# Sixteen dense products, which nothing reads, at the head of each step of the last mixers with a recurrent chunk

## What is computed

```
def _dsa_mixer(q, c, iq, ik, iw, w_uk, rel_bias):      # per block of 128 queries
    dots = jnp.einsum('bqhd,bsd->bqhs', iqb, ik) * idx_scale
    score = jnp.einsum('bqh,bqhs->bqs', iwb * w_scale, jax.nn.relu(dots))
    score = jnp.where(admissible[None], score.astype(jnp.float32), -jnp.inf)
    _, sel = lax.top_k(score, k_sel)                    # 256 keys of up to 2048
...
    logits = (jnp.einsum('bqhr,bqkr->bqhk', ql, c_sel).astype(jnp.float32) * scale
              + jnp.swapaxes(bias, -1, -2).astype(jnp.float32))
    p = jax.nn.softmax(logits, axis=-1).astype(c.dtype)
    return jnp.einsum('bqhk,bqkr->bqhr', p, c_sel)

def _hgrn2_mixer(q, f_raw, v, lb):                      # per chunk, with a carried state
    scores = jnp.einsum('bhtk,bhsk,bhtsk->bhts', qn, kn, decay)
    o = (jnp.einsum('bhts,bhsv->bhtv', scores, vn)
         + jnp.einsum('bhtk,bhkv->bhtv', qn * jnp.exp(bn), state))
    state = (jnp.exp(b_last[:, :, 0, :])[..., None] * state
             + jnp.einsum('bhsk,bhsv->bhkv', kn * jnp.exp(b_last - bn), vn))
```

## Time and profile before

| what | value |
|---|---|
| time, median of 3 runs | 5533.85 us (5530.03 to 5535.99) |
| time of the profiled execution | 5534.45 us |
| its span in the profile | 5532.8 us |
| mean granted TensorE clock | 0.837 of full speed |
| TensorE, VectorE, ScalarE busy over the span | 82%, 47%, 34% |
| steps k = 0 to 15 of the last mixers | 3719.6 to 5197.8 us, 27% of the span |

### The profile page before, as it was taken

The page is one execution under the profiler, slowest core; times in us unless marked ns, Lnnn a source line. Parts: engine busy times, 40 slices in busy tenths (PEclk is TensorE's granted clock), DMA queues, the critical chain, the costliest instruction groups (busy, mean ns, idle before and its releaser), DMA issues. The chain is left out here.

```text
span 5532.8 us, 59862 instructions
## 1 busy us (share of the span) xinstructions
PE 4531.4 (82%) x20858; PEld 3279.3 (59%) x20858; DVE 2604.0 (47%) x5329; ACT 1896.7 (34%) x3847; POOL 689.8 (12%) x724
## 2 busy tenths in 40 slices
PE   3994999984478888989798999966688877877689
PEld 3883777774367677777445888853344444545544
DVE  3011444454555554444111111127898888888433
ACT  3011322233322332333111101013677767777511
POOL 3001111110000000000000000003223333444300
PEclk7997999996687877777899999976577887877699
DMA  3514666664100000000322121120000001011032
GB/s 126 167 64 150 215 215 209 206 219 137 40 32 22 22 22 13 20 22 3 112 87 82 63 80 68 65 73 12 25 20 18 18 18 35 18 35 35 31 135 87
DMA packets 227869, 417.63 MB, mean 75 GB/s; under 512 B 36905, under 2 KB 100041, under 8 KB 227401
## 3 DMA queue, kind: packets, MB, share of 16 engines
q1 hardware_dynamic: 227568, 413.81, 22.2%
HBM read 292.08 MB, written 121.65 MB: 75 GB/s over the span
## 5 line engine op out<-in xcount | busy, mean ns | idle before, releaser
L2382 PE MATMUL ds_big<-ds_ikT,ds_iqT 64*128 64x512 f32 (+3 forms) x640 | 385.5, 753 | 88.0 <-ACT ds_iqT L2359 57.0
L2893 POOL TENSOR_TENSOR ds_E<-ds_bT 128x256 f32<-128x256 f32 x112 | 72.1, 643 | 2966.3 <-ACT ds_bT L2862 2782.7
L292 DVE COPY g_stage<-g_acc 128x512 f32<-128x512 f32 (+2 forms) x96 | 61.6, 642 | 784.9 <-PE g_acc L280 784.9
L278 PE MATMUL g_acc<-g_ws_hi,second_hT_hi 128*128 128x512 f32 (+1 forms) x1024 | 385.0, 376 | 11.7 <-DVE g_ws_lo L313 11.7
L279 PE MATMUL g_acc<-g_ws_lo,second_hT_hi 128*128 128x512 f32 (+1 forms) x1024 | 384.7, 376 | 0.0
L280 PE MATMUL g_acc<-g_ws_hi,second_hT_lo 128*128 128x512 f32 (+1 forms) x1024 | 384.6, 376 | 0.0
L549 PE MATMUL mm_big<-mm_gw_hi,mm_ghT_hi 128*128 128x512 f32 (+1 forms) x768 | 318.8, 415 | 43.2 <-PEq L134 42.7
L2445 DVE TENSOR_SCALAR_CACHE_REDUCE ds_eq<-ds_hi,ds_num 128x2048 uint16<-128x2048 uint16 (+13 forms) x224 | 331.3, 1479 | 25.3 <-issue 3.0
L306 ACT ACTIVATE g_stage<-g_acc 128x512 f32<-128x512 f32 (+2 forms) x96 | 53.7, 559 | 844.5 <-PE g_acc L280 844.5
L551 PE MATMUL mm_big<-mm_gw_hi,mm_ghT_lo 128*128 128x512 f32 (+1 forms) x768 | 300.4, 391 | 0.0
L550 PE MATMUL mm_big<-mm_gw_lo,mm_ghT_hi 128*128 128x512 f32 (+1 forms) x768 | 299.3, 390 | 0.0
(11 more groups left out here) (498 smaller groups left out, 9894.3 us busy)
## 6 DMA issues: line engine op xcount, KB each, us to landing
mm_ghT_hi<-turned SPq DMA_DIRECT2D x96, 512.0 KB, 4.2
mm_ghT_lo<-turned SPq DMA_DIRECT2D x96, 512.0 KB, 5.6
proj<-g_stage SPq DMA_DIRECT2D x160, 256.0 KB, 2.0
g_w<-in_w_in SPq DMA_DIRECT2D x80, 256.0 KB, 4.0
proj<-mm_gstage SPq DMA_DIRECT2D x80, 256.0 KB, 5.0
mm_x<-proj SPq DMA_DIRECT2D x64, 256.0 KB, 3.9
mm_graw<-in_w_in SPq DMA_DIRECT2D x40, 256.0 KB, 6.2
po_m<-mixed SPq DMA_DIRECT2D x16, 640.0 KB, 4.7
```

Of the source, the lines that this page charges most:

```text
L278: pe.matmul(sums, hT.hi[:, k, tile], wt.hi[:, k, 0:width], start=(k == 0), stop=False)
L2382: pe.matmul(big[:, n % 2, 0:wd], iqT[o, h // 2], b.ikT[o, x:x + wd], start=True, stop=True)\
```

## The change

A helper `dense` issues sixteen products on TensorE. Each takes the first 128 columns of the constants, read as bfloat16, as weights, and 512 columns of the same tile, read as bfloat16, as the moving operand, and writes all 512 columns of a bank of PSUM. Nothing waits for them, they wait for nothing, and nothing reads what they write. In `second_mixers` it is called ahead of all other work of TensorE in the steps k = 0 to 15, with bank 7 of `big`; in each of these steps that bank is written anew (L2972) before it is read.

```diff
+DENSE = 16
+
+
+def dense(pe, c, bank):
+
+
+    half = c.all[:, 0:GROUP // 2].bitcast(BF16)
+    for _ in range(DENSE):
+        pe.matmul(bank, half[:, 0:P], half, start=True, stop=True)
...
                 @block.tensor
                 def _(pe):
+                    if k < TILES:
+                        dense(pe, c, big[:, 7])
                     together(pe, "tensor", branches)
```

## The result

| | before | with the change |
|---|---|---|
| median of the runs timed together | 5534.92 us (4 runs) | 5579.77 us (4 runs, 5575.79 to 5591.14) |
| ratio | | 1.0086, 95% interval 1.0070 to 1.0102 |
| timed again, beside the last experiments | 5532.66 us (23 runs) | 5579.86 us (6 runs), ratio 1.0086 (1.0071 to 1.0101) |
| profiled execution, span | 5532.8 us | 5574.8 us |

The kernel is 0.86% slower, by 45 to 47 us. The forecast was 5579 us.

What follows compares the result with a forecast made beforehand. VectorE's list was taken to fill a step, its head hanging on a TensorE-ScalarE relay. ScalarE's 53 us less 11.5 slack gave 42, taken as 45; with 0 for k = 0 to 2, 5579 us, range 5550 to 5608 (8 in 10).

Steps and rivals of the forecast that it cites:

- The head is a relay, and the burst stands ahead of it: Heads of k = 3 to 15: TensorE and ScalarE wait on each other, so the burst delays ScalarE by 53 us in all.
- cold heads: 8 of the 13 heads, met at 1.2 GHz: burst 6.0 us, 1.4 given back, ScalarE 4.6 us later each.
- warm ones: 5 of the 13 heads, met at 2.4 GHz: burst 4.2 us, 0.9 given back, ScalarE 3.3 us later each.
- The give-back: L2692 and L2697 behind the burst run at 2.4 GHz: 1.4 us saved in a cold head, 0.9 in a warm one.
- The slack ahead of L2942 is taken off: VectorE starts L2942 after L2851 has ended; this slack, 11.5 us over 13 steps, cuts its delay from 53 to 42 us.
- Nothing takes the delay back: Behind L2942 VectorE is nearly full, so its 42 us delay reaches the step's end; later waits may raise it, at most to 53.
- k = 0 to 2 count nothing: The three steps before: slack of 7.9 and 4.7 us hides the burst in k = 1 and 2; k = 0 counts 0, 3 us either way.
- The warm head: Rival: the clock stays up until the chunk's products, some 15 us behind the entry, giving 5500 to 5526 us; chance 7%.
- Absorption: Rival: VectorE's slack and later waits in the step soak up the delay, 0 to 11 us, 5534 to 5545 us; chance 8%.
- the clock that does not rise: Rival: the burst's mostly zero operand does not raise the clock, bursts take 6.9 us, nothing given back, 5612 us; chance 8%.

## Why the prediction was right, point by point

- **The head is a relay, and the burst stands ahead of it.** Right. ScalarE's net delay was forecast as 53 us in 13 steps and measured 52.1 at L2624. Both terms of it were off and cancelled: I had a burst of 6.0 us in cold heads and 4.2 in warm ones; from the head to L2703 it was 5.2 us in the mean of the former and 4.9 of the latter (66.7 us in all, forecast 69). I had misread: the 2.9 us there are the length of a stretch at 1.2 GHz that began some 2 us into unbroken products (TensorE was at work from 854.82 on), and no measure of how long a burst stays cold. In the eight cold heads the clock rose 2.7 to 5.5 us behind the entry, 3.7 in the mean, where I had 5; the products start 0.43 us apart ahead of that and 0.216 behind it. Of the five heads that had been warm, k = 9 and 14 met the clock already down, in k = 10 and 11 it fell in the first 0.4 us, and only k = 12 ran all sixteen at 2.4 GHz. The give-back was 66.7 - 52.1 = 14.6 us, forecast 15.7.
- **The slack ahead of L2942 is taken off.** Right at that place (41.0 us measured, 42 forecast) and wrong as a step of the sum. This is the step that failed. At L2955, some 12 us later in each step, VectorE was 51.5 us late, which is the relay's whole delay, near the 53 that I had given as an upper bound. The 10.5 us between the two figures come in at the evictions of index products (7.2) and at L2664 (3.4), waits that the sum of the prediction left out; its 45 took in 3 us for them. The kernels with 4, 8 and 32 products and with zeros show the same: the delay at L2955 is the relay's to within 1.5 us, whatever the slack did at L2942. With the gates first L2942 is out of the way, and VectorE is late at L2955 all the same, there by 62 of the relay's 100 us, as much as the first eviction of index products.
- **Nothing takes the delay back.** Nearly right, and this hid the error: the profiled run lost 51.5 us by L2955 and gave 8 back later. Most of that is in k = 5 and 6, which were 4.1 and 4.8 us late at L2955 and end 0.3 us early and 0.9 late. Late in k = 5, in the kernel before and then with the change (columns as in the earlier trace rows):

```profile
4310.00:4363.80 53.80, 45.72 (x229) 29.96 (x228) 46.11 (x80) 27.84 (x58) 17.86 (x16) 0.89 0.00 1
```

```profile
4313.90:4367.50 53.60, 45.09 (x250) 29.80 (x249) 49.59 (x86) 31.69 (x63) 20.57 (x21) 0.99 0.00 1
```

  The granted clock was 0.99 there instead of 0.89, and VectorE and ScalarE get 3.5 and 3.9 us more work done in the same length. My reading is that it depends on where the clock's rises and falls happen to lie in the steps, and that a burst does not give time back as a rule; that is not shown: from L2955 to the end the delay of the kernel with zeros grew by 3.8 us and that with four by 4.9, while those with eight and thirty-two lost 2.7 and 8.2. The second profile of the change repeats the first (51.6 us at L2955, 43.7 at the end), so it belongs to the kernel and is no scatter between executions. Why it falls so for a given kernel is open; no run isolates it. That the steps came out 43.8 us longer and the time near the forecast is therefore partly luck.
- **k = 0 to 2 count nothing.** Right: -0.3 us in all, with -1.1 in k = 0 and L2942's slack in k = 1 and 2 reduced from 7.95 and 4.73 us to 5.55 and 3.84. In k = 0 the granted clock was 1.00 from 4.2 to 11.0 us behind the entry, and TensorE's work there gave back what the burst had cost.
- **The rivals.** The warm head gained nothing: in the changed kernel the clock was down again before the index products in ten of the 13 steps and fell during them in the other three. The page "TensorE: Matmul & The Clock Gate" of the Trainium skill, section "HAM oscillation — how this bites in real kernels", says that idle gaps between bursts of TensorE's work take its higher clock away again. This trace agrees on the clock: it rose with the burst in 12 of the 13 heads and was at 0.50 again 10 to 13 us behind the entry, during the wait ahead of the index products or just behind it. With products in the waits it stayed up longer, and then it was worth 10 us in a profile and nothing measurable in the median. My 8 to 35 us for that case were too much: VectorE has its own work, and TensorE then waits 17 us more for GpSimd. Absorption was refuted by the 13 steps, 43.8 us longer, and by the time, and the clock that does not rise by the kernel with zeros.

## What to carry to other kernels

Before work is added ahead of a relay between two engines, follow the delay to every reader behind the relay, not to the first alone: slack counted at one reader protects that reader only. In the six profiles here with products at the heads of k = 3 to 15 in the old order, the kernel again and the zeros included, VectorE had the relay's whole delay at a later reader, some 12 us on; where ScalarE's order was changed, it had the smaller delay of the evictions that this reader waits for. Work that is to warm TensorE's clock belongs where TensorE waits anyway, and it can pay only where an engine that sets the end waits for TensorE: here 160 extra products in a wait were free, and even a clock held up behind them moved the time by less than the measurement can tell.

## What the runs showed that was not expected

- Products of zeros raised the granted clock like any others (L2703 at 273 ns in the median behind them). Behind four products L2708 still took 421 ns in the median, as L2697 before the change did; behind eight it took 275.
- Giving ScalarE the chunk's gates first, a move of three instructions, cost 69 us, since ScalarE then stood 5.6 us a step behind a transfer with the whole relay behind it.
- TensorE's busy time grew by 17 us over k = 3 to 15 though the bursts alone have 64.6 us there, and a product of each is missing: the rest of its work ran at the higher clock, 0.83 instead of 0.79 in the mean, and that saved the kernel nothing.
